# Two projections and two attentions, or one projection and one attention of 32 heads

## The chip, the core and the metric

The kernel runs on one core of a Trainium2 chip. Time is device time in microseconds (us), from the start of the program to its end. The engines run beside each other and synchronise by semaphores: PE (TensorE, matrix products and transposes), DVE (VectorE), ACT (ScalarE), POOL (GpSimd) and SP (SyncE), which issues most DMAs.

## The reference

A layer of an encoder is computed for two independent sets of 512 tokens (x_prompt and x_sample), 1024 numbers each. Cut to what matters:

```python
hn = rms_norm(x, norm_attn)
proj = hn @ w_in                          # 1184 columns
gq, gk, gv, c_q, c_kv, k_pe = split(proj) # 512, 128, 128 | 256, 128, 32
# A: 8 query heads, 2 key/value heads of 64: norm per head, rotary, attention
# B: q = norm(c_q) @ w_uq (8 heads of 64+32), k, v = norm(c_kv) @ w_ukv (8 heads of 64+64)
#    norm per head, rotary on the 32, k_pe shared by all heads, attention
x = x + concat(norm(oa), norm(ob)) @ w_o
x = x + expert_choice_moe(norm(x))        # 16 experts
```

The first 768 columns of a projected row are the *rows* of part A (queries, keys, values); the last 416 are the *latents* (c_q, c_kv, k_pe) of part B.

## The kernel before

Products are made in three parts: each operand is split into a high part (a rounded copy, made by ACT) and a low part (the rest, made by DVE), and PE multiplies high by high, high by low and low by high. So nearly every operand passes ACT and then DVE before PE can use it.

`project_and_attend` is called once per set. In it each engine runs its program of `project` and then that of `attend`, without a barrier between the two; a barrier and the clearing of semaphores stand at the end of each call (class `Phase`).

`project` handles four tiles of 128 tokens. For each of eight chunks of 128 weight rows PE multiplies three times into 512, 512 and 160 columns (L469); between the chunks stand the transposes of the next tile's x (L417), and for the tile before it the transposes of its normalised latents (L427, `latent_transposes`), the query product (L439, `queries`) and the key and value product (L448 to L450, `keys_values`). When all 1184 columns of a tile are done, ACT copies them from PSUM scaled (L538, `rows`) and squares them (L540); DVE sums the squares (L642 to L645, `row_stats`), POOL takes the inverse roots (L370 to L375, power of minus a half), DVE scales latents and rows (L652 to L656, `row_norms`). Then the latents are transposed and split (L516 on ACT, L635 on DVE). DVE rotates keys and queries of part A (L578 to L583, `rotations`), sums the squares of part B's queries and keys (L675 to L682, `mla_stats`), scales and rotates them (L689 to L692, `mla_norms`). In the first set the weights are also split (L486, L588) and the rotary tables made (L606, L611, `tables`). The second set uses the split weights again and starts with loading x (L326). The order on each engine is written out by hand in a loop over tiles at the end of each program.

`attend` goes through 64 units, four query blocks of 16 heads, as a pipeline written out over u. For unit u: scores on PE (L835 to L840), their maximum on DVE (L993), the exponential on ACT (L938), transposes on PE (L849), the split of the transposed probabilities on ACT (L948) and DVE (L989), and the product with the values on PE (L867, L870, for pairs of units). Queries and keys of a head are transposed (L824) and split (L913 to L919 on ACT, L963 to L974 on DVE) some units ahead, by the table `due`; values are split on POOL (L803, L805). Head outputs are transposed, scaled (L1004) and stored to DRAM in three parts (L784). DVE does what is left of the last two tiles' `mla_norms` and `mla_stats` at u = 1, 2 and 6. In the second set ACT and POOL also split the output weights w_o (L953, L791, L793), which SP loads in four pieces, the last two behind the use of the first two.

After both sets `route` (output projection, router) and `experts` follow; they wait for the stored outputs.

Of the kernel before, what the change touches and what calls it, by code (L numbers as in the profile page):

```python
# [59 lines left out]
STATS = QH + KVH + 3  # L60

# [55 lines left out]
def build(nc, a, out):  # L117
# [6 lines left out]
    h2_rows = h2_dram.rearrange("(t p) d -> t p d", p=P)  # L124

    with ExitStack() as ctx:
# [34 lines left out]
        k["affT"] = Map(shared_at)("affT", [EXPERTS, T * P])  # L161
        rows = Map(arena)
# [18 lines left out]
        temps["grow"] = tm("grow", [G_ROWS, P])  # L181
        temps["small"] = tm("small", [P, 128])
        latents_at = tm.at
# [3 lines left out]
        squares_at = tm.at  # L187
# [5 lines left out]
        w["whi"] = wm("whi", [P, KD, D_IN], F32R)  # L193
        w["wlo"] = wm("wlo", [P, KD, D_IN], F32R)
# [5 lines left out]
        w_end = wm.at  # L200
# [4 lines left out]

        am = Map(temps_at)
        att = {}
        att["hi"] = [[am(f"{n}hi{i}", [P, SEQ], F32R) for i in range(2)] for n in "qk"]
        att["lo"] = [[am(f"{n}lo{i}", [P, SEQ], F32R) for i in range(2)] for n in "qk"]

        assert am.at <= sq_at
        att["p"] = [Map(sq_at + i * SEQ * 4)(f"prob{i}", [P, SEQ]) for i in range(2)]
        am = Map(gains_at)
        att["nmax"] = am("nmax", [P, HEADS * TS])
        att["sum"] = am("psum", [P, HEADS * TS])
        att["rsum"] = am("rsum", [P, HEADS * TS])
        assert am.at <= latents_at - 512
        am = Map(latents_at)
        att["ot"] = am("ot", [VD, SEQ])
        att["otv"] = am("otv", [VD, SEQ])  # L220
        assert am.at <= squares_at
        att["pthi"] = [Map(at)(f"probThi{i}", [P, TS, 2 * P], F32R) for i, at in enumerate((shared_at, squares_at))]
        assert squares_at + 2 * TS * P * 4 <= weights_at
# [3 lines left out]
        wo["hi"] = om("wohi", [P, KD, D], F32R)  # L227
        wo["lo"] = om("wolo", [P, KD, D], F32R)
        om2 = Map(om.at)
        wo["raw"] = om("woraw", [P, 4, D])  # L230
        assert om.at <= end
        am = Map(w_end)
        att["p"].append(am("prob2", [P, SEQ]))
        att["ptlo"] = [am(f"probTlo{i}", [P, TS, 2 * P], F32R) for i in range(2)]
        att["v"] = [am(f"v{i}", [P, TS, 2, VD], F32R) for i in range(2)]
        assert am.at <= end
# [4 lines left out]
        assert om2.at <= end  # L241
        om3 = Map(temps_at)
        om4 = Map(om2.at)
        wo["o"] = [om3("o0", [P, D]), om3("o1", [P, D]), om4("o2", [P, D])]
        wo["x"] = [om3("xr0", [P, D]), om3("xr1", [P, D]), om4("xr2", [P, D])]
        assert om4.at <= end
# [34 lines left out]
        for s in range(SETS):  # L281
            project_and_attend(nc, s, a, x_dram, k, temps, w, att, wo, pj, q_rows, kv_rows, w_raw, uq_raw, ukv_raw,
                               ps, banks, o_rows, o_stored, wo_loaded)
# [4 lines left out]
def project(phase, s, a, x_dram, k, tp, w, pj, q_rows, kv_rows, w_raw, uq_raw, ukv_raw, ps, banks, o_stored):  # L288
# [4 lines left out]

    first = s == 0
# [3 lines left out]
    ssx, rx = small[:, 0:TS], small[:, TS:2 * TS]  # L298
    ssa, rsa = small[:, 8:8 + STATS], small[:, 24:24 + STATS]
    ssk, rsk = small[:, 40:40 + MH], small[:, 48:48 + MH]  # L300
    ssb, rsb = small[:, 56:56 + 2 * MH], small[:, 72:72 + 2 * MH]
    xt_ps = [banks(0, 1), banks(1, 1)]
    pj_ps, c_ps, u_ps = banks(2, 3)[:, 0:D_IN], banks(5, 1)[:, 0:3 * P], banks(6, 2)
    chunks = [(0, 512), (512, 1024), (1024, D_IN)]
# [6 lines left out]
    w_loaded, u_loaded = [sem(f"w_loaded{i}") for i in range(KD if first else 0)], sem("u_loaded")  # L311
# [4 lines left out]
    proj_done, pj_done, c_normed = sem("proj_done"), sem("pj_done"), sem("c_normed")  # L316
# [3 lines left out]
    stat_a, stat_k, stat_b = sem("stat_a"), sem("stat_k"), sem("stat_b")  # L320
    ra_done, rk_done, rb_done = sem("ra_done"), sem("rk_done"), sem("rb_done")
    vsteps, psteps = sem("vector_steps"), sem("pool_steps")

    def sync_program(sp):
        def load_x(t):
            sp.dma_start(x[t % 2][:], x_dram[TS * s + t]).then_inc(x_loaded[t % 2], 16)  # L326

        if first:
            sp.wait_ge(rows_set, 1)
            for row, name, n in ((G_ATTN, "norm_attn", D), (G_QA, "mla_q_a_norm", Q_LORA),  # L330
                                 (G_KVA, "mla_kv_a_norm", KV_LORA), (G_OUT, "out_norm_a", C_K),
                                 (G_OUT + C_K // P, "out_norm_b", MH * VD)):
                sp.dma_start(tp["grow"][row:row + n // P, :], a[name].rearrange("(r c) -> r c", c=P)).then_inc(gains_loaded, 16)
            for row, name in ((G_QN, "mla_q_nope_norm"), (G_KN, "mla_k_nope_norm")):
                sp.dma_start(tp["grow"][row:row + 1, 0:NOPE], a[name].rearrange("(r c) -> r c", r=1)).then_inc(gains_loaded, 16)
            load_x(0)
            for i in range(KD):
                if i == KD // 2:
                    load_x(1)
                sp.dma_start(w_raw[:, i, :], a["w_in"][i * P:(i + 1) * P, :]).then_inc(w_loaded[i], 16)  # L340
            sp.dma_start(uq_raw[:], a["mla_w_uq"].rearrange("(k p) n -> p k n", p=P)).then_inc(u_loaded, 16)
            sp.dma_start(ukv_raw[:], a["mla_w_ukv"]).then_inc(u_loaded, 16)
        else:
            load_x(0)
            load_x(1)
        for t in range(2, TS):
            sp.wait_ge(xt_ready, 2 * (t - 1))
            sp.wait_ge(ssx_done, t - 1)
            load_x(t)

    def gpsimd_program(pool):
        steps = Steps(pool, psteps)
        if first:
            pool.memset(tp["grow"][:], 1.0).then_inc(rows_set, 1)
            steps.did(pool.memset(k["minus_half"][:], -0.5))
            steps.did(pool.memset(k["ident"][:], 0.0))
            steps.wait()
            pool.affine_select(out=k["ident"][:], in_=k["ident"][:], compare_op=ALU.not_equal, fill=1.0,
                               base=0, pattern=[[-1, P]], channel_multiplier=1).then_inc(ident_ready, 1)
            pool.dma_start(k["invn"][:], a["invn"]).then_inc(const_loaded, 16)  # L360
            pool.dma_start(k["tab"][:], a["tab"].rearrange("(i p) c -> p i c", p=P)).then_inc(tables_loaded, 16)
            at = 0
            for name, n in (("gqa_q_norm", HD), ("gqa_k_norm", HD), ("mla_q_pe_norm", PE_D), ("mla_k_pe_norm", PE_D)):
                pool.dma_start(tp["gb"][:, at:at + n], a[name].partition_broadcast(P)).then_inc(tables_loaded, 16)
                at += n
            pool.wait_ge(const_loaded, 16)

        def inverse_root(dst, src, done):

            steps.did(pool.tensor_scalar(src, src, 1.0, EPS, ALU.mult, ALU.add))  # L370
            steps.wait()
# [1286 lines left out]
```

## Time and profile before

| what | us |
|---|---|
| median of three runs | 1241.86 (1241.02 to 1241.93) |
| profiled execution | 1240.62 |
| its span | 1238.8 |
| first set: tiles 0 to 3, tail, attention | 16.0 to 90.2, to 112.3, to 249.0 |
| to the second set's first product | to 257.0 |
| second set: tiles, tail, attention | to 330.2, to 353.1, to 497.5 |
| routing, experts | to 1238.8 |

PE is busy for 88% of the span, DVE for 74%, ACT for 62%, POOL for 22%. Matrix products are pipelined, so that their durations overlap: their price is the distance from one start to the next. Rows of the timeline merge equal instructions (x3); the bracket at the end gives how long the engine stood before them, and what ended that. The granted clock is TensorE's, as a share of 2.4 GHz; it has two levels, 1.2 and 2.4 GHz.

### The profile page before, as it was taken

The page shows a single profiled execution, that of the slowest core. Times are in us where ns is not written, and L with a number is a line of the kernel's source. Part 1 is how long each engine was busy: PE and PEld are TensorE (multiplying, and loading weights), DVE is VectorE, ACT ScalarE, POOL GpSimd, SP SyncE. Part 2 cuts the span into 40 slices and gives each one's busy share as a digit, 9 for nine tenths or more (in the row PEclk, how much of TensorE's full clock was granted, in tenths as well). Part 3 has the DMA queues.
Part 4 walks back from the last instruction along what each step waited for, and adds up shares of the span by engine and source line. Part 5 has one row for each costly group of instructions (what it writes and reads, how often), then busy time and mean ns, then how long its engine had stood idle before and what let it go on. Part 6 is the DMA issues. An engine that isn't in the chain of part 4 may idle for free. (4 is left out here: it accounts for less than half of the span.)

```text
span 1238.8 us, 16803 instructions
## 1 busy us (share of the span) xinstructions
PE 1094.8 (88%) x5699; PEld 913.9 (74%) x5699; DVE 920.0 (74%) x1236; ACT 767.5 (62%) x1005; POOL 270.9 (22%) x272
## 2 busy tenths in 40 slices
PE   5995899879758899599953999999999999999996
PEld 4874678768547787488842788888888888888885
DVE  4567999815678897133576788988888888898883
ACT  5433788723348887233242777777777877777772
POOL 1244001103455521022123011101111111110211
PEclk9996999989979999799975999999999999999999
DMA  7000000020010000566216899999999999999992
GB/s 266 18 1 1 1 1 35 19 85 1 1 69 35 35 35 18 206 209 222 97 56 212 330 361 393 393 395 395 395 395 395 394 394 410 394 395 396 395 360 34
DMA packets 70109, 255.40 MB, mean 206 GB/s; under 512 B 5736, under 2 KB 7867, under 8 KB 70059
## 3 DMA queue, kind: packets, MB, share of 16 engines
q1 hardware_dynamic: 62730, 229.07, 47.6%
q0 software_dynamic: 7328, 25.68, 7.3%
q8 instruction: 29, 0.48, 0.2%
q14 instruction: 22, 0.17, 0.0%
HBM read 233.76 MB, written 20.97 MB: 206 GB/s over the span
## 5 line engine op out<-in xcount | busy, mean ns | idle before, releaser
L1570 DVE TENSOR_TENSOR lo<-raw,hi 128x2048 fp32r<-128x2048 f32 x189 | 427.8, 2290 | 63.8 <-ACT hi L1505 43.5
L1505 ACT ACTIVATE hi<-raw 128x2048 fp32r<-128x2048 f32 x192 | 364.5, 1918 | 72.3 <-PE ps L1422 65.7
L1420 PE MATMUL ps<-hi,xehi 128*128 128x512 f32 x512 | 202.0, 395 | 3.2 <-DVE xelo L1575 3.2
L1422 PE MATMUL ps<-hi,xelo 128*128 128x512 f32 x512 | 200.7, 392 | 0.0
L1421 PE MATMUL ps<-lo,xehi 128*128 128x512 f32 x512 | 200.7, 392 | 0.0
L1420 PEld LDWEIGHTS ps<-hi,xehi 128*128 128x128 f32 x512 | 97.1, 190 | 23.6 <-issue 2.9
L1422 PEld LDWEIGHTS ps<-hi,xelo 128*128 128x128 f32 x512 | 96.9, 189 | 20.2
L1421 PEld LDWEIGHTS ps<-lo,xehi 128*128 128x128 f32 x512 | 97.0, 189 | 19.7
L938 ACT ACTIVATE prob<-ps,nmax 128x512 f32<-128x512 f32 x128 | 87.9, 687 | 23.8 <-DVE nmax L993 21.6
L849 PE MATMUL ps<-ident,prob 128*128 128x128 f32 x512 | 79.7, 280 | 20.2 <-DVE probTlo L989 19.9
L849 PEld LDWEIGHTS ps<-ident,prob 128*128 128x128 f32 x512 | 61.4, 143 | 46.9 <-issue 22.8
L1434 PE MATMUL ps<-hi,hthi 128*128 128x512 f32 x240 | 94.7, 395 | 0.0
L1436 PE MATMUL ps<-hi,htlo 128*128 128x512 f32 x240 | 93.5, 390 | 0.0
L1435 PE MATMUL ps<-lo,hthi 128*128 128x512 f32 x240 | 93.4, 389 | 0.0
L1360 POOL COPY take<-idxT 128x1 uint32 (+1 forms) x15 | 12.8, 852 | 366.8 <-PE ps L1405 366.8
L989 DVE TENSOR_TENSOR probTlo<-ps,probThi 128x512 fp32r<-128x512 f32 x128 | 86.6, 678 | 5.0 <-ACT probThi L948 4.6
L993 DVE TENSOR_REDUCE nmax<-ps 128x1 f32<-128x512 f32 x128 | 86.7, 678 | 4.9 <-PE ps L836 4.7
L948 ACT ACTIVATE probThi<-ps 128x512 fp32r<-128x512 f32 x128 | 75.8, 592 | 22.2 <-PE ps L849 22.1
L867 PE MATMUL ps<-probThi,v 128*128 128x256 f32 x256 | 58.3, 311 | 0.6 <-DVE probTlo L989 0.6
L372 POOL TENSOR_TENSOR small<-small,minus_half 128x13 f32<-128x13 f32 (+2 forms) x24 | 57.1, 2381 | 2.0
L469 PE MATMUL ps<-whi,xhi 128*128 128x512 f32 (+1 forms) x192 | 49.6, 368 | 8.9 <-DVE wlo L588 5.4
L1246 DVE TENSOR_TENSOR x<-ps,xr 128x512 f32<-128x512 f32 x16 | 10.3, 686 | 59.8 <-PE ps L1150 59.8
(213 smaller groups left out, 2047.2 us busy)
## 6 DMA issues: line engine op xcount, KB each, us to landing
raw<-in_w_gate SPq DMA_DIRECT2D x64, 1024.0 KB, 7.3
raw<-in_w_up SPq DMA_DIRECT2D x64, 1024.0 KB, 7.3
raw<-in_w_down SPq DMA_DIRECT2D x64, 1024.0 KB, 7.7
w_raw<-in_w_in SPq DMA_DIRECT2D x8, 592.0 KB, 12.3
x<-in_x SPq DMA_DIRECT2D x8, 512.0 KB, 4.1
woraw<-in_w_o SPq DMA_DIRECT2D x4, 1024.0 KB, 4.9
o<-attention_out SPq DMA_DIRECT2D x8, 512.0 KB, 3.8
xr<-in_x SPq DMA_DIRECT2D x8, 512.0 KB, 4.7
```

What stands on the lines that cost most here:

```text
L849: last = pe.transpose(ps[:, T_BANKS[u % 2], cols], att["p"][u % 3][:, cols], k["ident"][:])
L938: act.activation(att["p"][v % 3][:], ps[:, S_BANKS[v % 3], :], ACT.Exp, bias=att["nmax"][:, v:v + 1], accum_out=att["sum"][:, v:v + 1]).th ...
L989: dve.tensor_tensor(ptlo[v // 2 % 2][:, :, cols], ps[:, T_BANKS[v % 2], :].rearrange("p (a c) -> p a c", a=TS), pthi[v // 2 % 2][:, :, col ...
L993: dve.tensor_reduce(att["nmax"][:, u:u + 1], ps[:, S_BANKS[u % 3], :], AX.X, ALU.max, negate=True).then_inc(max_done, 1)
L1420: pe.matmul(ps[:, dst[n], :], xehi[:, c, :], hi[w][:, cols], start=c == 0, stop=False)
L1421: pe.matmul(ps[:, dst[n], :], xehi[:, c, :], lo[w][:, cols], start=False, stop=False)
L1422: last = pe.matmul(ps[:, dst[n], :], xelo[:, c, :], hi[w][:, cols], start=False, stop=c == KD - 1)
L1434: pe.matmul(ps[:, Y[n], :], hthi[:, f, :], hi[w][:, cols], start=f == 0, stop=False)
L1435: pe.matmul(ps[:, Y[n], :], hthi[:, f, :], lo[w][:, cols], start=False, stop=False)
L1436: last = pe.matmul(ps[:, Y[n], :], htlo[:, f, :], hi[w][:, cols], start=False, stop=f == KD - 1)
L1505: act.activation(hi[s][:], raw[s][:], ACT.Copy).then_inc(hi_done, 1)
L1570: dve.tensor_tensor(lo[s][:], raw[s][:], hi[s][:].bitcast(F32), ALU.subtract).then_inc(lo_done, 1)
```

## The change

Both sets are projected in one run of eight tiles and attended in one run of 32 heads (`g`, 16 of each set). In each tile the 416 latent columns are multiplied first, in a PSUM bank of their own, with their own copy, sums and root; then 512 row columns, then the last 256. The latents' transposes and the query product of a tile are in the same tile, the key and value product in the next. The first set's finished rows, queries and keys are stored to DRAM during tiles 4 to 7, and loaded back into the space of the projection weights when these are no longer read; the second set's stay where they are. The norms and rotations of the last tile move into the attention (u = 2, 5, 12, 15, 20). The output weights are loaded when the first set's outputs are stored, and split during heads 20 to 27. Several tiles of SBUF lie elsewhere. Cut to its core:

```diff
+LAT = D_IN - C_CQ
...
+    pj_dram = nc.dram_tensor("first_pj", [P, TS, C_CQ], F32).ap()
+    q_dram = nc.dram_tensor("first_q", [P, TS, MH * QK], F32).ap()
+    kv_dram = nc.dram_tensor("first_kv", [P, TS, MH * KB], F32).ap()
...
+        w["lathi"] = wm("wlathi", [P, KD, LAT], F32R)
+        w["latlo"] = wm("wlatlo", [P, KD, LAT], F32R)
+        latents_end = wm.at
+        w["rowhi"] = wm("wrowhi", [P, KD, C_CQ], F32R)
+        w["rowlo"] = wm("wrowlo", [P, KD, C_CQ], F32R)
...
+        first_rows = (bm("pjB", [P, TS, HEADS * VD]),)
+        assert bm.at <= latents_end
+        first_rows += (bm("q_rowsB", [P, TS, MH, QK]), bm("kv_rowsB", [P, TS, MH, KB]))
...
+            u = t - TS
+            if u >= 0:
+                sp.wait_ge(rows_ready, u + 1)
+                sp.dma_start(pj_dram[:, u, :], pj[:, u, 0:C_CQ]).then_inc(pj_stored[u], 16)
+                sp.wait_ge(mla_ready, u + 1)
+                sp.dma_start(q_dram[:, u, :], q_rows[:, u].rearrange("p h c -> p (h c)")).then_inc(mla_stored[u], 16)
+                sp.dma_start(kv_dram[:, u, :], kv_rows[:, u].rearrange("p h c -> p (h c)")).then_inc(mla_stored[u], 16)
...
+        pjB, qB, kvB = att["rows"][0]
+        for u in range(TS):
+            sp.wait_ge(pj_stored[u], 16)
+        sp.wait_ge(lat_done, T)
+        sp.dma_start(pjB[:, :, 0:C_CQ], pj_dram).then_inc(pj_back, 16)
+        for u in range(TS):
+            sp.wait_ge(mla_stored[u], 32)
+        sp.wait_ge(proj_done, T)
+        sp.dma_start(qB[:].rearrange("p t h c -> p t (h c)"), q_dram).then_inc(mla_back, 16)
+        sp.dma_start(kvB[:].rearrange("p t h c -> p t (h c)"), kv_dram).then_inc(mla_back, 16)
...
+        x_root(0)
+        x_root(1)
+        for t in range(T):
+            if t >= 1:
+                row_roots(t - 1)
+                if t >= 2:
+                    query_roots(t - 1)
+            latent_roots(t)
+            if t == 1:
+                query_roots(0)
+            if t >= 1:
+                key_roots(t - 1)
+                if t + 1 < T:
+                    x_root(t + 1)
+        row_roots(LAST)
...
+        def chunk(t, c, group):
+            name, lo, up, dst = group
+            for lhs, part in ((xhi[t % 2], "hi"), (xhi[t % 2], "lo"), (xlo[t % 2], "hi")):
+                last = pe.matmul(dst, lhs[:, c, :], w[name + part][:, c, lo:up],
+                                 start=(c == 0 and part == "hi" and lhs is xhi[t % 2]),
+                                 stop=(c == KD - 1 and lhs is xlo[t % 2]))
+            return last
...
+        def project_latents(t):
+            pe.wait_ge(xlo_done, 2 * t + 2)
+            pe.wait_ge(lat_copied, t)
+            for c in range(KD):
+                last = chunk(t, c, groups[0])
+            last.then_inc(lat_done, 1)
+
+        def project_queries(t):
+            pe.wait_ge(row_copied, t)
+            for c in range(KD):
+                chunk(t, c, groups[1])
+
+        def project_keys_values(t):
+            for c in range(KD):
+                last = chunk(t, c, groups[2])
+            last.then_inc(proj_done, 1)
...
+        for t in range(1, T):
+            project_latents(t)
+            if t == 1:
+                latent_transposes(0)
+                x_transposes(2)
+                queries(0)
+                project_queries(1)
+                keys_values(0)
+            else:
+                keys_values(t - 1)
+                if t + 1 < T:
                     x_transposes(t + 1)
-                if c == 4 and t:
-                    latent_transposes(t - 1)
-                if c == 6 and t:
-                    queries(t - 1)
-                pe.wait_ge(xlo_done, 2 * t + c // 4 + 1)
-                if t and c == 0:
-                    pe.wait_ge(pj_done, 2 * t - 1)
-                if first and t == 0:
-                    pe.wait_ge(wlo_done, c + 1)
-                for lhs, rhs in ((xhi[t % 2], "whi"), (xhi[t % 2], "wlo"), (xlo[t % 2], "whi")):
-                    for lo, up in chunks:
-                        last = pe.matmul(pj_ps[:, lo:up], lhs[:, c, :], w[rhs][:, c, lo:up],
-                                         start=(c == 0 and rhs == "whi" and lhs is xhi[t % 2]),
-                                         stop=(c == KD - 1 and lhs is xlo[t % 2]))
-            last.then_inc(proj_done, 1)
-            if first and t == 0:
-                pe.wait_ge(wlo_done, KD + 3)
-            if t:
-                keys_values(t - 1)
-        latent_transposes(TS - 1)
-        queries(TS - 1)
+                project_queries(t)
+            latent_transposes(t)
+            project_keys_values(t)
+            queries(t)
...
+                act.activation(w["lathi"][:, i, :], w_raw[:, i, C_CQ:D_IN], ACT.Copy, scale=gain).then_inc(whi_done, 1)
+                act.activation(w["rowhi"][:, i, :], w_raw[:, i, 0:C_CQ], ACT.Copy, scale=gain).then_inc(whi_done, 1)
...
+        x_high(0)
+        split_weights()
+        x_high(1)
+        latent_rows(0)
+        rows(0)
+        for t in range(1, T):
+            latent_rows(t)
+            if t == 1:
+                latents_high(0)
+                x_high(2)
+                queries(0)
+                keys_values(0)
+            else:
+                keys_values(t - 1)
+                if t + 1 < T:
+                    x_high(t + 1)
+            latents_high(t)
             rows(t)
-            if t >= 1:
-                keys_values(t - 1)
-        latents_high(TS - 1)
-        queries(TS - 1)
+            queries(t)
...
         x_low(0)
-        if first:
-            split_weights()
-        for t in range(TS):
+        split_weights()
+        x_low(1)
+        latent_stats(0)
+        row_stats(0)
+        latent_norms(0)
+        tables()
+        for t in range(1, T):
             if t >= 2:
-                mla_stats(t - 2)
-            if t + 1 < TS:
-                x_low(t + 1)
-            if t >= 1:
-                latents_low(t - 1)
-                rotations(t - 1)
+                query_stats(t - 1)
+            row_norms(t - 1)
+            rotations(t - 1)
+            latent_stats(t)
+            if t == 1:
+                latents_low(0)
+                x_low(2)
+                query_stats(0)
+                latent_norms(1)
+                key_stats(0)
+            else:
+                key_stats(t - 1)
+                latent_norms(t)
+                if t + 1 < T:
+                    x_low(t + 1)
+            latents_low(t)
+            mla_norms(t - 1)
             row_stats(t)
...
+    def wait_for_rows(engine, g):
+        if g == 0:
+            engine.wait_ge(pj_back, 16)
+        elif g == QH:
+            engine.wait_ge(mla_back, 32)
+        elif g == HEADS:
+            engine.wait_ge(rows_ready, T)
+        elif g == HEADS + QH:
+            engine.wait_ge(mla_ready, T)
...
+        for s in range(SETS):
+            for h0, h1 in O_PARTS:
+                cols = slice(h0 * VD, h1 * VD)
+                sp.wait_ge(o_done, HEADS * s + h1)
+                sp.dma_start(o_rows[TS * s:TS * (s + 1), :, cols].rearrange("t p d -> p t d"),
+                             att["rows"][s][0][:, :, cols]).then_inc(o_stored, 16)
+            if s == 0:
+                sp.wait_ge(o_stored, 16 * len(O_PARTS))
+                for i in range(KD // 2):
+                    if i >= 2:
+                        sp.wait_ge(wo_lo, 2 * (i - 1))
+                    sp.dma_start(wo["raw"][:, 2 * (i % 2):2 * (i % 2) + 2, :],
+                                 a["w_o"].rearrange("(k p) n -> p k n", p=P)[:, 2 * i:2 * i + 2, :]).then_inc(wo_loaded, 16)
...
+        split_after = {HEADS + GROUP: (0, 1), HEADS + QH: (2, 3), HEADS + QH + 1: (4,), HEADS + QH + 2: (5,),
+                       HEADS + QH + 3: (6,), HEADS + QH + 4: (7,)}
+        keys = [g for kind, g in preps if kind == "k"]
+        pool.wait_ge(proj_done, T)
...
+            if u >= SECOND and u % 4 == 2 and 4 <= (u - SECOND) // 4 < KD + 4:
+                i = (u - SECOND) // 4 - 4
...
+            if u == 2:
+                query_stats(T - 1)
+            elif u == 5:
+                key_stats(T - 1)
+            elif u == 12:
+                row_norms(T - 1)
+            elif u == 15:
+                rotations(T - 1)
+            elif u == 20:
+                mla_norms(T - 1)
```

## Rows read from the trace of the kernel before

**Rows 1.** Windows by stage, whole core: length, busy time and instructions per engine, granted clock.

```profile
90.20:112.30 22.10, 8.90 (x30) 7.25 (x30) 14.20 (x43) 6.33 (x10) 10.56 (x11) 0.64 0.00 1
112.30:249.00 136.70, 122.36 (x833) 102.03 (x831) 121.27 (x223) 105.44 (x236) 15.47 (x24) 0.97 0.04 13
249.00:257.00 8.00, 1.99 (x9) 1.59 (x9) 0.69 (x1) 1.21 (x3) 0.00 (x0) 0.55 0.58 197
...
353.10:497.50 144.40, 124.70 (x833) 103.99 (x831) 122.89 (x223) 112.41 (x244) 58.05 (x40) 0.96 0.11 41
```

**Rows 2.** Timeline: start, duration, engine, line, operation, count, idle time before and releaser.

```profile
34.70 0.78 PE L469 MATMUL ps<-whi,xhi 128*128 128x512 f32 x3 [1.43 <-ACT pj L538]
...
53.39 0.78 PE L469 MATMUL ps<-whi,xhi 128*128 128x512 f32 x3
...
97.41 0.90 PE L427 MATMUL ps<-ident,pj 128*128 128x128 f32 x3 [7.19 <-DVE pj L653]
...
106.16 0.59 ACT L915 ACTIVATE khi<-ps 64x512 fp32r<-64x512 f32 x1 [1.09 <-PE ps L824]
...
110.64 0.68 DVE L963 SCALAR_TENSOR_TENSOR qhi<-ps,qhi 64x512 fp32r<-64x512 f32 x1 [1.78 <-ACT qhi L913]
...
254.38 1.97 PE L417 MATMUL ps<-ident,x 128*128 128x128 f32 x8 [5.85 <-DMA x<-in_x]
```

**Rows 3.** Timeline of PE late in tile 3: starts of following products give their spacing.

```profile
85.75 0.73 PE L469 MATMUL ps<-wlo,xhi 128*128 128x512 f32 x3
...
86.32 0.74 PE L469 MATMUL ps<-whi,xlo 128*128 128x512 f32 x3
...
88.89 0.39 PE L449 MATMUL ps<-ukvlo,chi 128*128 128x512 f32 x1
...
89.12 0.39 PE L450 MATMUL ps<-ukvhi,clo 128*128 128x512 f32 x1
```

**Rows 4.** Timeline of DVE (tile 1, then the first tail); POOL's group by form, tiles 1 to 3.

```profile
31.59 1.28 DVE L627 TENSOR_TENSOR xlo<-ps,xhi 128x512 fp32r<-128x512 f32 x2
...
91.43 0.42 DVE L642 TENSOR_REDUCE small<-sq 128x1 f32<-128x256 f32 x1 [4.66 <-ACT sq L540]
...
92.78 0.68 DVE L689 TENSOR_TENSOR kv_rows<-kv_rows,small 128x512 f32<-128x512 f32 x1
...
95.57 0.43 DVE L583 TENSOR_TENSOR q_rows<-q_rows,ra 128x256 f32<-128x256 f32 x1
...
101.13 0.39 DVE L578 TENSOR_TENSOR ra<-pj,gkp 128x8 f32<-128x8 f32 x4
...
105.14 0.29 DVE L583 TENSOR_TENSOR pj<-pj,ra 128x128 f32<-128x128 f32 x1
...
L372 POOL TENSOR_TENSOR small<-small,minus_half 128x16 f32<-128x16 f32 x2 | 5.9, 2969 | 0.2
```

**Rows 5.** Timeline of DVE: first and last of the eight pieces of the rotary tables.

```profile
37.16 0.42 DVE L606 TENSOR_TENSOR gq<-tab,gb 128x256 f32<-128x256 f32 x1
...
39.81 0.49 DVE L611 TENSOR_TENSOR gkp<-tab,gb 128x32 f32<-128x32 f32 x4
```

**Rows 6.** Windows of L938 (an exponential and its read-back per unit): length, ACT busy, count.

```profile
114.10:141.35 27.25, 9.31 (x24) 0.87 0.00 1
156.80:179.80 23.00, 9.34 (x24) 1.00 0.00 1
203.50:227.20 23.70, 9.32 (x24) 1.00 0.07 24
```

**Rows 7.** Timeline of ACT; then DMA issues: destination, source, queue, count, size, time to landing.

```profile
406.84 1.15 ACT L953 ACTIVATE wohi<-woraw,gcol 128x1024 fp32r<-128x1024 f32 x1 [3.72 <-DMA woraw<-in_w_o]
...
woraw<-in_w_o SPq DMA_DIRECT2D x4, 1024.0 KB, 4.9
```

**Rows 8.** Timeline of POOL: the scaling of 13 sums beside a busy and an idle DVE.

```profile
92.94 0.60 POOL L375 TENSOR_TENSOR small<-small,invn 128x13 f32<-128x13 f32 x1 [6.16 <-DVE small L645]
...
277.34 0.22 POOL L375 TENSOR_TENSOR small<-small,invn 128x13 f32<-128x13 f32 x1 [11.66 <-DVE small L645]
```

More of the change, by code:

```diff
@@ new lines, in sync_program @@
+        for row, name in ((G_QN, "mla_q_nope_norm"), (G_KN, "mla_k_nope_norm")):
+            sp.dma_start(tp["grow"][row:row + 1, 0:NOPE], a[name].rearrange("(r c) -> r c", r=1)).then_inc(gains_loaded, 16)
+        load_x(0)
+        for i in range(KD):
+            if i == KD // 2:
+                load_x(1)
+            sp.dma_start(w_raw[:, i, :], a["w_in"][i * P:(i + 1) * P, :]).then_inc(w_loaded[i], 16)
+        sp.dma_start(uq_raw[:], a["mla_w_uq"].rearrange("(k p) n -> p k n", p=P)).then_inc(u_loaded, 16)
@@ L347, in sync_program @@
+        sp.dma_start(ukv_raw[:], a["mla_w_ukv"]).then_inc(u_loaded, 16)
+        for t in range(2, T):
             sp.wait_ge(xt_ready, 2 * (t - 1))
@@ L352, in gpsimd_program @@
         steps = Steps(pool, psteps)
[L353 to L366, printed above, removed]
@@ L368, in inverse_root @@
-        def inverse_root(dst, src, done):
-            steps.did(pool.tensor_scalar(src, src, 1.0, EPS, ALU.mult, ALU.add))
+        pool.memset(tp["grow"][:], 1.0).then_inc(rows_set, 1)
+        steps.did(pool.memset(k["minus_half"][:], -0.5))
+        steps.did(pool.memset(k["ident"][:], 0.0))
+        steps.wait()
+        pool.affine_select(out=k["ident"][:], in_=k["ident"][:], compare_op=ALU.not_equal, fill=1.0,
+                           base=0, pattern=[[-1, P]], channel_multiplier=1).then_inc(ident_ready, 1)
@@ L421, in latent_transposes @@
             pe.wait_ge(c_normed, u + 1)
-            if u == 0 and first:
+            if u == 0:
                 pe.wait_ge(gcol_ready, 1)
@@ new lines, in project_queries @@
+        def project_queries(t):
[6 more added lines that the diff above has]
+            last.then_inc(proj_done, 1)
+        x_transposes(0)
+        for c in range(KD):
+            if c == 2:
+                x_transposes(1)
+            if c % 4 == 0:
+                pe.wait_ge(xlo_done, c // 4 + 1)
+            pe.wait_ge(wlo_done, c + 1)
+            latent = chunk(0, c, groups[0])
+            if c == KD - 1:
+                latent.then_inc(lat_done, 1)
+            chunk(0, c, groups[1])
+            last = chunk(0, c, groups[2])
@@ L734, in attend @@
     STEPS = 8
-    units = [(h, i) for h in range(HEADS) for i in range(TS)]
+    ALL = SETS * HEADS
+    units = [(g, i) for g in range(ALL) for i in range(TS)]
     NU = len(units)
+    SECOND = HEADS * TS
     qhi, khi = att["hi"]
@@ L1017, in project_and_attend @@
[L1017 to L1023 removed]
+                                  rsum.unsqueeze(2).to_broadcast([P, TS, VD]), ALU.mult).then_inc(o_done, 1)
```

544 lines of the change are left out of this document (256 added, 288 removed).

## The prediction

> **What bounds the kernel now.** I read the windows by stage first. Each set runs through the same stages: four projection tiles, a tail of about 22 us in which hardly anything runs, and an attention of about 140 us; between the sets lie 8.0 us more [rows 1]. In the first tail TensorE is busy for 8.9 of 22.1 us, and its granted clock is 0.64 there, so much of the little that it does runs at the lower of its two levels, 1.2 GHz [rows 1]; the second tail looks alike. In the gap between the sets it is busy for 2.0 of 8.0 us and waits for the load of the second set's rows [rows 1, 2]. Inside the projections TensorE is the bound: tile 1 takes 53.39 − 34.70 = 18.7 us and PE stands still at its start only [rows 2]. Inside the attentions no engine is full: DVE is busy for 121.3 and PE for 122.4 of 136.7 us, and the rate is one unit per 1.92 us for the first head group (twelve exponentials in 23.0 us) and per 1.975 us for the second (twelve in 23.7 us) [rows 1, 6]. So heads cost 7.7 and 7.9 us, and sixteen of them 8 x 7.7 + 8 x 7.9 = 124.8 us. Everything behind 497.5 us (routing, experts) is not touched by the change, and starts when the last head's output is stored.
>
> The timeline of the tail tells what it is made of. PE's last product of tile 3 is followed by 7.2 us of waiting for the normalised latents (copy from PSUM, squares, sums, POOL's root, scaling), and only then come the query product, the rotations and the first head's preparation [rows 2]. Latents are a third of a tile's columns, but they wait for all columns.
>
> **The change part by part.** I rebuild the clock tile by tile; up to the first projection product the kernels are the same.
>
> *Tile 0.* PE's three products per weight row take 0.57 us for 512 + 512 + 160 columns, and one of 512 columns 0.23 us [rows 3]. The 160 columns therefore cost 0.11, more than their share. The new groups are 416, 512 and 256 columns: 0.19 + 0.23 + 0.12 = 0.54 us by share of columns. With 24 such rows a tile becomes 0.8 us shorter. In tile 0 PE also stood for 1.4 us until the copy of all 1184 columns had left PSUM [rows 2]; now it goes on with the latents' own bank. The weights are split in two pieces per row instead of one, on ACT and DVE; they end as late as before, since the loads set their pace. Tile 1 starts at 34.7 − 1.7 = 33.0 us (bounds 32.5 and 34.7).
>
> *Tile 1* gets a new wait. On PE the query product of tile 0 stands behind 4.6 us of latents and 1.2 us of transposes (eleven at the 0.11 of the smallest product), so PE reaches it at 38.8. It needs the low half of tile 0's latents, and DVE's program has this behind the rotary tables, tile 0's row norms and its rotations. The tables took 37.16 to 40.3, the rotations of a tile 101.13 to 105.43, that is 3.1 and 4.3 us [rows 4, 5]. The tables start at about 36.7, a little earlier than before, and I get 36.7 + 3.1 + 0.9 (row norm) + 4.4 + 0.7 (latent sums) + 0.6 (low half) = 46.4. PE stands for 7.6 us, and ACT's copies of queries behind it too. After 7.2 us of standing in the old tail the granted clock was low [rows 1, 2], so I add 2 us (the 2.1 us of query products once more). The tile then carries two query products and lasts to about 63 us. If DVE were faster here the wait would be 5 us, no less.
>
> *Tiles 2 to 7.* The old tile less 0.8 us and less the short stand at its start is 17.7 us of PE work. What has to fit under it is DVE's list. In the old tail DVE went once through everything it does for one tile except x's low half: 91.43 to 105.43, 14.0 us with 1.5 us of waiting [rows 4]. With x's low half (1.28 [rows 4]) that is 13.8 us. Now it waits twice for POOL: for the root of ten sums and for that of three latent sums. A root of 16 sums took 2.97 us, 0.19 per column [rows 4], so these are about 2.4 and 1.5 us with their preparation; 1.1 and 0.7 us of other sums stand in their shadow, and POOL's five roots together take some 10 us of a tile. The round is 13.8 + 1.3 + 0.8 + about 1 for hand-overs = 17 us against PE's 17.7. It fits by some 0.7 us. I take 18.2 for tile 2, which still catches up, 17.7 for tiles 3 to 6 and 16.9 for tile 7, which transposes no further x. PE ends the last query product at 63 + 18.2 + 70.8 + 16.9 = 168.9. The lower bound is the same; the upper is 18.7 per tile, the old pace, +6 us.
>
> *DRAM.* 1.5 + 1.5 + 2.5 MB go out and come back. The stores are issued by SP behind waits for finished rows, ahead of the next x load; these rows are done a tile earlier, so x isn't late. The read-back of the first part is issued when the last latents are out of PE, 12 us before the first head needs it. One megabyte took 4.9 us [rows 7]; at that rate 1.5 MB need 7.4 us. Cover remains 4 us; without any cover it would cost 7.4. The query and key rows (4 MB, 20 us) are needed at unit 28, more than 50 us later. ACT waits for the stores before it overwrites rows, four tiles later: free.
>
> *The one tail.* After the last query product ACT passes twice over its 768 columns (1.7 us by the 0.59 that 512 took), then the first head is prepared: from the first key copy at 106.16 to the end of the query's low half at 111.3 took 5.2 us [rows 2]. First scores: 168.9 + 1.7 + 5.2 = 175.8. The rest of the last tile (second set's norms and rotations) is not needed before head 16 and moves into units 2 to 20.
>
> *Attention in one run.* Two times 124.8 = 249.6 us of heads, plus filling and draining once. In the first set the old run took 136.7: 124.8 + 4.2 lost at the start (27.25 us for twelve units instead of 23.0) + 7.7 for filling and draining [rows 1, 6]. The 4.2 came from DVE blocks between the units: the 3.2 us of query and key norms [rows 4] at unit 6 hits a running pipeline, the others fall into its filling. Now the block of rotations (4.3) and row norm (0.8) at 12 to 15, and the norms (3.5 with the key copy) at 20, all hit a running pipeline; with 1.1 for the start that is 9.2 us (bounds: 1.5 if the pipeline had slack for them, 11 if all counts). The second set was 7.7 us longer than the first; 3.7 of it is one ACT wait for the output weights' second load [rows 1, 7]. These splits sit at the same distance from each other as before, so this wait stays, with 1 us more for the slow end; I take 4.7 (bounds 3.7 and 7.7). SP issues the weight loads between the two sets' stores; a store waits behind them, for which nobody waits. Sum: 249.6 + 7.7 + 9.2 + 4.7 = 271.2, so the last output is written at 447.0 instead of 497.5. Gain 50.5 us.
>
> The profiled execution took 1240.62 us (span 1238.8), so the sum gives 1190.1; the median of the runs is 1241.86, 1.24 above it, which makes **1191 us**.
>
> **A rule against it.** DVE and POOL now work closer together in every tile. In the trace, POOL's scaling of 13 sums took 0.60 us while DVE multiplied two SBUF tiles and 0.22 us while it didn't [rows 8]. The Trainium skill says why that may grow: by "SBUF — State Buffer", section "Who interferes with whom", a DVE instruction with two SBUF inputs and a GpSimd instruction that reads SBUF exclude each other for a whole instruction. The trace agrees in kind with its 0.38 us of difference; the sum above goes without it, and the first rival prices it.
>
> **The rivals.** *DVE and POOL set the pace of the tiles.* Against PE's 17.7 the round has only 0.7 us to spare. If each of POOL's two roots on the round (three instructions each) loses 0.4 us to DVE, the round is 17 + 2.4 = 19.4 and tiles 2 to 7 cost 1.7 each: +10 to +11, 1202 us. For it speaks that 0.60 [rows 8]; against it that on the round DVE mostly waits for POOL and so leaves it alone.
>
> *The tail stays long.* If the read-back or the row work is late, the first head comes up to 15 us later, as in the old tail (22 instead of 7): 1206 us. Against it: the old tail's 7.2 us of standing was for latents [rows 2], which now end under the row products.
>
> *Slower.* The single mechanism is PE standing once in every tile for the latents, and restarting at the lower clock. At the end of tile 3 this cost 7.2 us [rows 2], and some 2 more at 1.2 GHz. Seven tiles with 9.2 us are 64 us, more than the 50.5 gained: 1255 us. It decides from a round longer by 5.9 us than I have it, 23 instead of 17. No row shows such a round.
>
> *The DVE blocks are free.* The pipeline absorbs what it lost before: −7.7 us, 1183 us.
>
> **How the numbers follow.** Forecast 1191 (1184 to 1198): 0.65. First rival 1202: 0.17. Long tail 1206: 0.07. Slower 1255: 0.03. Free blocks 1183 or a little less: 0.08. The range runs from 1182 to 1205. A difference of 0.2% (2.5 us) is about what a measurement of this kernel can tell from none. All cases but one are faster by far more: faster 0.96, same 0.01, slower 0.03.
>
> **What would show it.** In the profile after: one gap of about 8 us on PE in tile 1 in front of the query product, released by the latents' low half on DVE; tile starts 17.7 us apart from tile 3 on, with PE idle for under 0.5 us in each; first scores near 176; three visible stretches of exponentials in the first six heads, 4 and 3 us long; 7.7 and 7.9 us per head after that, with one ACT wait of 3 to 4 us at the output weights; last head's output near 447. I am wrong in size if tiles are 19 us or more apart, and wrong in kind if PE waits for latents in every tile or the first head waits for its rows from DRAM.

## The result and the profile after

The changed kernel takes 1191.01 us (median of four runs, 1189.97 to 1194.04) beside 1241.56 us for the kernel before on the same chip: a ratio of 0.960, 95% interval 0.958 to 0.961. The forecast was 1191 us. The profiled execution has a span of 1189.1 us against 1238.8, so 49.7 us less.

The windows of the changed kernel answer [rows 1]: three steady tiles, the last tile, the one tail, and the one attention.

```profile
80.06:97.63 17.57, 17.57 (x102) 16.21 (x102) 13.73 (x43) 8.52 (x14) 9.83 (x12) 1.00 0.33 113
97.63:115.22 17.59, 17.59 (x102) 16.21 (x102) 13.72 (x43) 8.51 (x14) 9.83 (x12) 1.00 0.34 113
115.22:132.80 17.58, 17.58 (x103) 16.22 (x102) 13.74 (x43) 8.52 (x14) 9.83 (x12) 1.00 0.15 61
150.40:167.30 16.90, 16.89 (x94) 15.24 (x94) 12.66 (x41) 6.38 (x10) 9.08 (x10) 1.00 0.32 106
167.30:175.56 8.26, 3.21 (x14) 2.31 (x13) 3.43 (x5) 3.16 (x5) 3.24 (x4) 0.81 1.00 426
175.56:448.50 272.94, 248.38 (x1675) 207.49 (x1673) 238.53 (x436) 217.61 (x480) 68.61 (x59) 0.96 0.09 32
```

PE's busy time equals the length of each steady tile, so PE is the bound of the projection and never waits in these tiles. What were tails of 22.1 and 22.9 us to the first scores, and 8.0 us between the sets, is one tail of 6.3 us to the first scores (8.3 us to the first exponential, the fifth window). So 46.7 of the 49.7 us come from tails and gap, 6.2 from the one attention (274.9 us instead of 136.7 + 144.4), and about 1 from the start and the part behind; the eight tiles give back 4.3 (151.7 instead of 74.2 + 73.2 us), the stand in tile 1 included. The last column of the fifth window, and the DMA share of 1.00 before it, show the read-back of part B's queries and keys from DRAM; part A's rows were read in tile 7.

The timeline of the changed kernel (PE, one row of ACT, one of DVE) shows most of the marks that the forecast named:

```profile
32.82 0.42 PE L493 MATMUL ps<-wlathi,xhi 128*128 128x416 f32 x1 [1.73 <-ACT pj L585]
45.78 0.69 PE L476 MATMUL ps<-uqhi,chi 128*128 128x384 f32 x1 [6.99 <-DVE clo L716]
171.55 0.63 PE L942 MATMUL ps<-ident,pjB 128*64 128x128 f32 x4 [3.65 <-DVE klo L1086]
173.58 0.80 PE L955 MATMUL ps<-khi,qhi 128*128 128x512 f32 x1 [1.40 <-DVE qhi L1081]
...
380.54 1.15 ACT L1070 ACTIVATE wohi<-woraw,gcol 128x1024 fp32r<-128x1024 f32 x1 [3.62 <-DMA woraw<-in_w_o]
448.06 0.42 DVE L1123 TENSOR_TENSOR pj<-ps,rsum 128x256 f32<-128x256 f32 x1 [0.47 <-PE ps L998]
```

One wait of 7.0 us for the latents' low half in tile 1; first scores at 173.6; the wait for the output weight as in [rows 7]; the last head's output done at 448.5, where it was 497.5. No row of PE names the read-back as its releaser. Behind that point the program takes 740.6 us, before 741.3, so nothing of the gain is lost later.

### The profile page after: what moved, and what is told of

The parts are those of the page before. It is cut to its first block and busy times, and to the rows that moved or that the text cites. A ratio compares the mean times of both kernels' runs of the same rounds, so it can differ in the third digit from the quotient of the medians.

```text
span 1189.1 us, 16857 instructions
## 1 busy us (share of the span) xinstructions
PE 1076.0 (90%) x5699; PEld 908.9 (76%) x5699; DVE 922.1 (78%) x1244; ACT 771.5 (65%) x1029; POOL 271.8 (23%) x280
## 5 line engine op out<-in xcount | busy, mean ns | idle before, releaser
L397 POOL TENSOR_TENSOR small<-small,minus_half 128x1 f32<-128x1 f32 (+4 forms) x40 | 65.1, 1628 | 3.3
L1369 DVE TENSOR_TENSOR x<-ps,xr 128x512 f32<-128x512 f32 x16 | 10.3, 686 | 59.0 <-PE ps L1273 59.0
L1559 PEld LDWEIGHTS ps<-hi,htlo 128*128 128x128 f32 x240 | 45.0, 188 | 9.4
```

The lines of the kernel that those rows point to most:

```text
L1559: last = pe.matmul(ps[:, Y[n], :], htlo[:, f, :], hi[w][:, cols], start=False, stop=f == KD - 1)
```

## The experiments

All are edits of the changed kernel. Times are medians, and differences are taken to its 1191.0 us; the kernel before stood at 1241.7 and 1240.8 us beside the two groups of runs, within 0.8 us of its 1241.6.

**Latents with their rows.** The order of columns is undone, the single run kept; the latents keep their own bank, copy and sums. Shown is PE's list of a tile, shortened; ACT's, DVE's and GpSimd's follow it, and the norms of tile 6 go into the attention too.

```diff
-            project_latents(t)
-            keys_values(t - 1); x_transposes(t + 1)
-            project_queries(t)
-            latent_transposes(t)
-            project_keys_values(t)
-            queries(t)
+            for c in range(KD):
+                if c == 2: x_transposes(t + 1)
+                if c == 4: latent_transposes(t - 1)
+                if c == 6: queries(t - 1)
+                chunk(t, c, groups[0]); chunk(t, c, groups[1]); chunk(t, c, groups[2])
+            keys_values(t - 1)
+        latent_transposes(LAST)
+        queries(LAST)
```

> The changed kernel with the latents' part of the change undone: both sets are still projected in one run and attended in one run, but each tile's 1184 columns are made chunk by chunk as in the kernel before, and its latents are transposed and multiplied in the next tile. Theory (most of the gain comes from having one projection and one pipeline instead of two; latents first pays only at the end of the projection and costs a stand in tile 1): no stand of 7.0 us in tile 1, but the copy of a whole row holds tile 1 back by about 1.9 us, the latents of the last tile cost 7 to 9 us of waits plus 2.0 us of products before the first key preparation, and one more set of norms (about 4 us) lies in the first heads: about 1201 us, 1196 to 1207. Rival (latents first carries most of the gain, because each tile's pace depends on it): over 1215 us.

Measured: 1199.3 us, ratio 0.965 (0.964 to 0.967), 8.3 us more than the changed kernel. So 42.3 of the 50.6 us come with the single run (and the latents' own bank), 8.3 with the order of columns. PE's timeline of this kernel shows the price of the old order, paid once at the end of the projection and no longer twice:

```profile
34.33 0.43 PE L489 MATMUL ps<-wlathi,xhi 128*128 128x416 f32 x1 [2.27 <-ACT pj L593]
163.83 0.90 PE L460 MATMUL ps<-ident,pj 128*128 128x128 f32 x3 [5.19 <-DVE pj L709]
165.95 0.69 PE L472 MATMUL ps<-uqhi,chi 128*128 128x384 f32 x1 [1.22 <-DVE clo L694]
176.27 0.80 PE L929 MATMUL ps<-khi,qhi 128*128 128x512 f32 x1 [1.40 <-DVE qhi L1055]
```

There is no 7 us stand in tile 1, but 5.2 and 1.2 us at the end, and query products at the clock's lower level behind them. First scores come at 176.3, only 2.7 us later than in the changed kernel; heads 0 to 7, where the norms of tile 6 now lie too, take 3.6 us more. What latents first would give two separate projections wasn't tried.

**The low half of the latents first.**

```diff
+            if t == 1:
+                latents_low(0)
+                latent_stats(1)
             row_norms(t - 1)
             rotations(t - 1)
-            latent_stats(t)
+            if t >= 2:
+                latent_stats(t)
             if t == 1:
-                latents_low(0)
                 x_low(2)
```

> One move in VectorE's list of tile 1: latents_low(0) (0.55 us) and latent_stats(1) go ahead of row_norms(0) and rotations(0) (0.8 and 4.3 us). Theory (the prediction's: the stand of 7.0 us before queries(0) is the order of VectorE's list, and the 12 products behind it run at the lower of TensorE's two clocks): chi is there at 39.1 us and the tables end at 39.3, so queries(0) starts near 39.9 instead of 45.8 and its 12 products take 2.0 instead of 3.9 us; tile 1 ends 6 to 8 us earlier and the kernel takes about 1184 us. Rival (VectorE's whole list sets tile 1, so that the same wait turns up before the latent transposes or the queries of tile 1): 0 to 2 us, 1189 to 1191 us.

Measured: 1185.0 us, ratio 0.954 (0.953 to 0.956), 6.0 us less. PE's row in front of the queries, which showed 6.99 us of waiting, is now:

```profile
39.99 0.44 PE L476 MATMUL ps<-uqhi,chi 128*128 128x384 f32 x1 [1.13 <-DVE clo L716]
```

The stand was the order of DVE's list, not its length: no other wait of that size comes up in its place (the longest in tiles 1 and 2 is 1.31 us).

**Extra work for VectorE in tiles 2 to 7**, three and six reductions (the same edit with 6 for 3):

```diff
             dve.wait_ge(row_squared, t + 1)
+            for _ in range(3 if t >= 2 else 0):
+                steps.did(dve.tensor_reduce(small[:, 100 + _:101 + _], sq[:, 0:C_V], AX.X, ALU.add))
```

> Three more reductions over 640 columns (0.74 us each, 2.2 us in all) in VectorE's list of each of tiles 2 to 7, ahead of row_stats; their results are not used. Theory (the prediction's figure: VectorE's round of a tile is 17.0 us against 17.7 on TensorE, 0.7 us to spare): each tile grows by 1.5 us, the kernel by 9 us to about 1200 us. Rival (VectorE is busy for 13.75 of a tile's 17.6 us, and most of its 3.85 us of idle time can take the work): 0 to 2 us more, 1191 to 1193 us.

> As with three, but six more reductions (4.4 us) in each of tiles 2 to 7. Theory (0.7 us to spare): each tile grows by 3.7 us, the kernel by 22 us to about 1213 us. Rival (all of VectorE's 3.85 us of idle time is to be had): 0.6 us in a tile, 4 us in all, about 1195 us. In between: the part of the idle time that is a wait within the chain from TensorE's products to VectorE's norms and back can't be had.

Measured: 1198.1 us with three (ratio 0.966, 0.965 to 0.968), 7.1 us more; 1217.5 us with six (0.982, 0.980 to 0.984), 26.5 us more. The windows of one steady tile with three, and of two with six, and the one row of PE in such a tile that waits, of either kernel:

```profile
100.49:119.24 18.75, 17.82 (x103) 16.14 (x102) 15.71 (x46) 8.51 (x14) 11.38 (x12) 1.00 0.32 106
```

```profile
113.87 0.55 PE L464 MATMUL ps<-ident,pj 128*128 128x128 f32 x3 [0.93 <-DVE pj L731]
```

```profile
80.66:104.17 23.51, 20.38 (x103) 18.73 (x103) 17.98 (x49) 8.51 (x14) 9.85 (x12) 0.85 0.32 115
104.17:126.35 22.18, 19.06 (x103) 17.41 (x102) 17.99 (x49) 8.52 (x14) 9.85 (x12) 0.92 0.21 65
```

```profile
96.20 0.90 PE L464 MATMUL ps<-ident,pj 128*128 128x128 f32 x3 [3.13 <-DVE pj L731]
```

Three reductions are 2.2 us (DVE's timeline has them from 100.35 to 102.54), and the tile grows by 18.75 − 17.58 = 1.17, so there were 1.05 us to spare, not 0.7, and not the 3.85 us that DVE is idle in a tile: most of that is its own waiting for ACT and POOL inside the chain to the normalised latents. Six are 4.4 us. Less the 1.05 that leaves 3.35, near the 3.13 us of waiting; yet the tiles grow by 5.9 and 4.6 us. The rest is the clock: after a stand of 3.1 us PE's granted clock in these tiles is 0.85 and 0.92 instead of 1.00, part of the tile at 1.2 GHz, and PE is busy for 2.8 and 1.5 us more with the same products.

**Three read-backs instead of one.**

```diff
-        sp.dma_start(pjB[:, :, 0:C_CQ], pj_dram).then_inc(pj_back, 16)
+        for _ in range(3):
+            sp.dma_start(pjB[:, :, 0:C_CQ], pj_dram).then_inc(pj_back, 16)
+            sp.wait_ge(pj_back, 16 * (_ + 1))
...
-            engine.wait_ge(pj_back, 16)
+            engine.wait_ge(pj_back, 48)
```

> The first set's query, key and value rows are read back from DRAM three times, one read after the other, and the first key preparation waits for the third. Theory (the way through DRAM is hidden, with 4 to 5 us to spare: the one read is issued at 155.2 us, takes 7.1 us and lands at 162.3, and the first key's transposes start at 167.3): a second and third read of 5 to 6 us each land near 173 us, so the first scores come 5 to 8 us later and the kernel takes about 1197 us. Rival (the read is not hidden but shares the end of the projection, and each repetition costs its whole 7 us): over 1203 us. Rival (far more to spare than seen): 1191 us.

Measured: 1201.5 us, ratio 0.968 (0.966 to 0.970), 10.5 us more. The DMA issues and the first key's transposes in this kernel:

```profile
pjB<-first_pj SPq DMA_DIRECT2D x3, 1536.0 KB, 7.3
...
178.31 1.06 PE L944 MATMUL ps<-ident,pjB 128*64 128x128 f32 x4 [9.66 <-DMA pjB<-first_pj]
```

Each read takes 7.3 us; my 5 to 6 us for the repeated ones was too little. Two more are 14.6 us, of which 9.66 show as waiting, so one read alone has 4.9 us to spare: hidden, as forecast (4 us). The rest of the 10.5 us lies ahead of the stand: in this execution the projection ends at 168.65 instead of 167.30 us, and 0.75 of that is there at the start of tile 1, which the edit doesn't touch. Behind the stand PE runs at its lower clock (the key's transposes take 1.06 us, 0.60 in the changed kernel), but that costs nothing: the first scores follow the transposes by 6.2 us here and by 6.3 there. That the stores cost nothing was not tried alone; PE's full tiles say it.

**The output weight one head later.**

```diff
-        split_after = {HEADS + GROUP: (0, 1), HEADS + QH: (2, 3), HEADS + QH + 1: (4,), HEADS + QH + 2: (5,),
-                       HEADS + QH + 3: (6,), HEADS + QH + 4: (7,)}
+        split_after = {HEADS + GROUP: (0, 1), HEADS + QH: (2, 3), HEADS + QH + 2: (4,), HEADS + QH + 3: (5,),
+                       HEADS + QH + 4: (6,), HEADS + QH + 5: (7,)}
...
-            if u >= SECOND and u % 4 == 2 and 4 <= (u - SECOND) // 4 < KD + 4:
-                i = (u - SECOND) // 4 - 4
+            late = (u - SECOND) // 4
+            if u >= SECOND and u % 4 == 2 and 4 <= late < KD + 5 and late != 8:
+                i = late - 4 if late < 8 else late - 5
```

> The last four splits of the output weight (ScalarE's and GpSimd's) come one head later, in heads 25 to 28 instead of 24 to 27. Theory (ScalarE stands 3.6 us for the output weight's last rows and the heads behind it wait with it: heads 24 and 25 take 11.5 and 9.9 us): with the rows there before they are asked for, the kernel takes 3.5 to 5 us less, about 1187 us. Rival (the time is GpSimd's, which is late with the values of the next head because of its own two instructions for each split): 0 to 1 us less, 1190 to 1191 us.

Measured: 1186.3 us, ratio 0.957 (0.955 to 0.958), 4.7 us less. ACT's split no longer waits:

```profile
383.20 1.15 ACT L1071 ACTIVATE wohi<-woraw,gcol 128x1024 fp32r<-128x1024 f32 x1
```

Heads 24 and 25, which took 11.5 and 9.9 us from first exponential to first exponential, take 7.9 each. In the changed kernel:

```profile
373.73 0.70 ACT L1056 ACTIVATE prob<-ps,nmax 128x512 f32<-128x512 f32 x1
385.20 0.69 ACT L1056 ACTIVATE prob<-ps,nmax 128x512 f32<-128x512 f32 x1
395.13 0.69 ACT L1056 ACTIVATE prob<-ps,nmax 128x512 f32<-128x512 f32 x1
```

Not all of that is the wait: head 25 takes 8.3 us in the kernel with the early low half, whose program is the same there. The wait came from the buffer: the fourth split's low half leaves it at 375.6 us in the changed kernel, the next rows are loaded only then, and 4.9 us [rows 7] later, at 380.5, ACT goes on.

**The last tile's norms and rotations in pieces**: 18 of them at units 13, 15 and so on to 47, the ten of the other heads' norms at 61, 64 and so on to 88.

```diff
-            elif u == 12:
-                row_norms(T - 1)
-            elif u == 15:
-                rotations(T - 1)
-            elif u == 20:
-                mla_norms(T - 1)
+            elif u in pieces:
+                pieces[u]()
```

> The norms and rotations of the last tile, which VectorE does in three blocks at units 12, 15 and 20 of the attention, are cut into 28 pieces of 0.1 to 0.7 us, one at every second or third unit from 13 to 88. The same arithmetic, in pieces. Theory (a block stops the pipeline of heads because it is longer than the slack of a unit; VectorE has 0.8 us of idle time in a head): pieces hide, heads 3 and 5 go back from 12.3 and 12.1 to about 8 us, and the kernel takes 7 to 10 us less, about 1183 us. Rival (VectorE lies in the loop of each unit, so every microsecond put into it costs about a microsecond, in pieces or not): 0 to 3 us less, 1188 to 1191 us.

Measured: 1186.8 us, ratio 0.956 (0.954 to 0.958), 4.2 us less: between the two. ACT's first exponentials of heads 3 to 6, of heads 20 and 21, and of the last head, in the changed kernel and then in this one:

```profile
199.38 0.69 ACT L1056 ACTIVATE prob<-ps,nmax 128x512 f32<-128x512 f32 x1
211.69 0.69 ACT L1056 ACTIVATE prob<-ps,nmax 128x512 f32<-128x512 f32 x1 [3.69 <-DVE nmax L1111]
220.62 0.69 ACT L1056 ACTIVATE prob<-ps,nmax 128x512 f32<-128x512 f32 x1
232.73 0.69 ACT L1056 ACTIVATE prob<-ps,nmax 128x512 f32<-128x512 f32 x1
...
342.84 0.69 ACT L1056 ACTIVATE prob<-ps,nmax 128x512 f32<-128x512 f32 x1
350.52 0.69 ACT L1056 ACTIVATE prob<-ps,nmax 128x512 f32<-128x512 f32 x1
...
434.22 0.69 ACT L1056 ACTIVATE prob<-ps,nmax 128x512 f32<-128x512 f32 x1
```

```profile
199.16 0.69 ACT L1131 ACTIVATE prob<-ps,nmax 128x512 f32<-128x512 f32 x1
207.33 0.69 ACT L1131 ACTIVATE prob<-ps,nmax 128x512 f32<-128x512 f32 x1
215.16 0.69 ACT L1131 ACTIVATE prob<-ps,nmax 128x512 f32<-128x512 f32 x1
222.93 0.69 ACT L1131 ACTIVATE prob<-ps,nmax 128x512 f32<-128x512 f32 x1
...
335.01 0.69 ACT L1131 ACTIVATE prob<-ps,nmax 128x512 f32<-128x512 f32 x1
343.80 0.69 ACT L1131 ACTIVATE prob<-ps,nmax 128x512 f32<-128x512 f32 x1
...
426.00 0.69 ACT L1131 ACTIVATE prob<-ps,nmax 128x512 f32<-128x512 f32 x1
```

Heads 3 and 5 fall from 12.3 and 12.1 to 8.2 and 7.8 us: the pieces there hide. Those at units 61 to 88 don't quite: heads 17 to 21 take 2.5 us more, head 20 8.8 instead of 7.7. From the first exponential of head 0 (175.56 and 175.35 us) to that of the last head it is 8.0 us less; but 2.0 of these are head 25, which holds no piece and took 7.9 to 9.9 us in executions with the same program there. So the edit gives some 6 us in the pipeline, and the span is 4.8 us shorter. The windows of the drain behind the last head's first exponential and of the output product, changed kernel first, show a difference behind it, too:

```profile
434.20:449.00 14.80, 10.26 (x75) 8.26 (x73) 9.74 (x19) 7.38 (x16) 0.61 (x1) 1.00 0.00 1
...
463.10:583.40 120.30, 115.47 (x614) 97.77 (x614) 51.31 (x106) 33.48 (x80) 20.89 (x43) 0.98 0.44 155
```

```profile
426.00:441.30 15.30, 11.48 (x75) 9.45 (x72) 9.55 (x19) 7.37 (x16) 0.59 (x1) 0.89 0.00 0
...
456.60:578.00 121.40, 116.55 (x614) 98.61 (x614) 51.33 (x106) 33.35 (x80) 20.89 (x43) 0.98 0.43 153
```

The same 75 products of the drain take PE 11.5 instead of 10.3 us at a granted clock of 0.89 instead of 1.00, and the 614 of the output product 1.1 us more. That this comes from the edit is not shown, and the other traces speak against it: of the nine versions of the changed kernel, the same in the drain, three (the changed kernel, latents with rows, three reductions) have 0.98 to 1.00 there, six 0.88 or 0.89, and the kernel before has 0.88. From the last head's first exponential to the end the nine take between 754.1 and 759.5 us; the changed kernel has 754.9, this one 758.3. Why the clock is lower in some executions stays open.

**All three together**, the pieces moved forward to units 13 to 58, `pieces = {13 + 5 * n // 3: ...}`:

> Three edits on the changed kernel at once: VectorE takes latents_low(0) ahead of the norms and rotations in tile 1, the last tile's norms and rotations are cut into 28 pieces between units 13 and 58 of the attention, and the last four splits of the output weight come one head later. Theory (the three stand at three places of the time line, and each gives what it gave alone: 6.0, 4.2 and 4.7 us): 14.9 us less, about 1176 us. Rival (the stage behind takes part of each again, because TensorE's clock falls when it stands): 8 to 11 us less, 1180 to 1183 us.

Measured: 1174.75 us, ratio 0.947 (0.946 to 0.949), 16.3 us less than the changed kernel. The three add up (6.0 + 4.2 + 4.7 = 14.9, and 1.4 us more), so no stage behind takes part of it again, and this version beats both kernels. Its window of the attention:

```profile
169.50:430.00 260.50, 243.06 (x1672) 202.15 (x1670) 236.43 (x445) 218.29 (x480) 69.11 (x59) 0.99 0.09 33
```

PE now is busy for 243 of 260 us, at a clock of 0.99.

## Why the prediction was right

The time was met, and the mechanism was the one argued: PE bounds the tiles, one tail and one gap go, DRAM is hidden, DVE's list makes a new wait in tile 1. That it was met to the microsecond is luck of signs: the projection was 2.2 us too long in the forecast, the attention 3.7 too short, the part behind 0.7 too long, and the 1.24 us from the profiled execution to the median, carried over from before, are 0.07 here (1190.94 and 1191.01). Term by term, from the changed kernel's profile (us):

| term | predicted | measured |
|---|---|---|
| tile 1 starts | 33.0 | 32.8 |
| stand before queries(0) ends | 46.4 | 45.8 |
| tile 1 ends | 63 | 61.9 |
| tile 2; tiles 3 to 6; tile 7 | 18.2; 70.8; 16.9 | 18.2; 70.3; 16.9 |
| from there to the first scores | 6.9 | 6.3 |
| first scores | 175.8 | 173.6 |
| DVE blocks, heads 0 to 7 above 7.7 | 9.2 | 10.9 |
| output weight, heads 24 and 25 above 7.9 | 4.7 | 5.6 |
| first scores to last output | 271.2 | 274.9 |
| last output | 447.0 | 448.5 |

*The projection*: of the 2.2 us, 1.1 lie in tile 1, half a microsecond each in tiles 3 to 6 together and in the first head's preparation. The stand in tile 1, its place, its releaser and its end were read off [rows 4, 5] within 0.6 us; moving the latents' low half ahead in DVE's list confirmed the cause. The start of tile 1 was right by two errors. PE was to go on with the latents' own bank; but there is one such bank, and PE stands 1.73 us until it is copied (the row at 32.82 above). ACT, with the next x before it in its list, begins that copy only at 32.07:

```profile
32.07 0.61 ACT L585 ACTIVATE pj<-ps,small 128x416 f32<-128x416 f32 x1 [0.16 <-issue]
```

And tile 0's last product ends at 31.1 us instead of 33.3, 2.2 us earlier, where 0.8 was forecast; why, no run shows. (The forecast's 1.7 for the start is also less than the 0.8 and 1.4 that it names.)

*The round of DVE* was put at 0.7 us less than PE's; it had 1.05. Right in kind, and the forecast hung on it: with 2.2 us more work per tile the kernel loses 7.1 us.

*The attention*: the largest part of the 3.7 us, 1.7, is the term of the blocks; 0.9 is that of the output weight, and some 1.1 lies in other heads and the drain. Much of it belongs to this execution: in the kernel with the early low half, whose program is the same from the first scores on, it is 272.1 us from these to the last output, 0.9 above the forecast. The 9.2 of the blocks is also a slip: its parts, 4.3, 0.8, 3.5 and 1.1, make 9.7. Two stretches came, not three: heads 3 and 5 take 4.6 and 4.4 us above 7.7, heads 0 and 4 each about 1. I had counted DVE's time alone. PE's timeline around head 3 in the changed kernel shows what I left out:

```profile
207.25 0.39 PE L956 MATMUL ps<-klo,qhi 128*128 128x512 f32 x1
211.20 1.09 PE L969 MATMUL ps<-ident,prob 128*128 128x128 f32 x4 [3.56 <-DVE probTlo L1107]
...
217.52 0.60 PE L969 MATMUL ps<-ident,prob 128*128 128x128 f32 x4
```

After 3.56 us of standing the same transposes take 1.09 instead of 0.60 us, until about 217: PE is at its lower clock for most of that (granted 0.53). I had added such a term in tile 1 and not here; the 1.1 us for the start was carried over from before without a cause. How much it costs differs between executions. Head 0 takes 8.75 us here and 7.61 in the kernel with the later output weight, which is the same up to there; the windows of these four microseconds, changed kernel first:

```profile
176.00:180.00 4.00, 4.00 (x15) 3.04 (x14) 0.70 (x2) 1.24 (x4) 0.00 (x0) 0.60 0.18 77
```

```profile
176.80:180.80 4.00, 3.40 (x19) 2.60 (x17) 1.88 (x4) 2.37 (x7) 0.00 (x0) 0.93 0.13 56
```

In the kernel with the early low half, heads 0 to 7 lose 8.7 us in all. So 9.2 lies between 8.7 and 10.9, for a reason that I hadn't given.

*The rivals.* DVE and POOL didn't set the pace. But the rule of the Trainium skill behind that rival ("SBUF — State Buffer", section "Who interferes with whom") shows elsewhere: DVE's timeline of the changed kernel at the last norms, beside POOL's:

```profile
220.19 0.88 DVE L779 TENSOR_TENSOR kv_rows<-kv_rows,small 128x512 f32<-128x512 f32 x1
221.00 1.22 DVE L781 TENSOR_TENSOR q_rows<-q_rows,small 128x512 f32<-128x512 f32 x1
```

```profile
220.61 1.06 POOL L919 TENSOR_TENSOR v<-kv_rowsB,v 128x256 fp32r<-128x256 f32 x1
```

Both DVE operations take 0.68 to 0.69 us in a tile, and POOL's 0.73 us at another head: here they lengthen each other, by 0.7 us on DVE. The trace agrees with the rule, at a place where the two engines don't wait for each other. In the tiles they mostly do; with three reductions one of POOL's roots runs beside DVE's norms and takes 2.09 instead of 0.56 us (so POOL's 11.38 instead of 9.83 us in the window above), but nobody waits for it there. The long tail didn't come: 6.3 us to the first scores. *The slower case* needed a round of 23 us. The kernel with six reductions went towards it, and its tiles grew by 4.6 to 5.9 us for 3.1 of waiting; the forecast's 2 us for each cold restart was of the right size. Free blocks: not free as blocks; in pieces some 6 of the 9 us that heads 3 and 5 lost come back.

## What to carry to other kernels

Merging two passes pays for each fill and drain that goes; count them in the windows by stage before arguing about the order inside (42 of 50 us here, against 8). When a step is moved forward on one engine, read the other engines' lists up to it: a 0.55 us operation behind 5 us of unrelated work cost 6 us. Work put into a running pipeline costs about its whole length as a block (4.6 and 4.4 us here for blocks of 5.1 and 3.5), with a lower clock besides; in pieces it costs less, but not nothing.

## What was not expected of the hardware

The idle time of an engine isn't its slack: DVE was idle for 3.85 of 17.6 us in a tile, and 1.05 could be had. A stand of PE of 3.1 us in a tile cost 1.5 to 2.8 us more than itself, by a granted clock of 0.85 and 0.92. And executions of the same instructions differ: head 0 took 8.75 or 7.61 us at a clock of 0.60 or 0.93 over four of them, head 25 between 7.9 and 9.9 us, and the part behind the last head's first exponential between 754.1 and 759.5 us. So a difference of 2 or 3 us in one stage of one trace is not yet the edit's.
